# A decoder trunk with expert rows on TensorE: in the attention stages, the attention's matmuls are put ahead of the expert rows that are due

## What is computed

```python
h = rms(x) @ w_in                         # q, k, v, latents, convolution channels, gates
y_d = diff_attention(...)                 # 4 heads, two maps each: softmax(q0 k0) - lam * softmax(q1 k1), times v
y_m = mla(...)                            # 8 heads of 96, causal softmax, times v
y_c = short_conv(...)
x += (g0 * (y_d @ W_d) + g1 * (y_m @ W_m) + g2 * (y_c @ W_c)) @ w_out
# PEER: per token 8 heads x 16 experts, from 16384
act = gelu(sum(u_tab[expert] * hc))       # one dot per expert row
x += sum(gate * act * v_tab[expert])      # one weighted row per expert
x += sigmoid(rms(x) @ w_ple_gate) * (p @ w_ple_proj)
```

## Time and profile before

| | us |
|---|---|
| median of 3 runs | 3959.45 (3955.41 to 3967.53) |
| the profiled execution's own time | 3950.54 |
| its span in the trace | 3948.7 |
| TensorE, VectorE, ScalarE busy in it | 2984.8, 2583.0, 1447.1 |
| mean granted TensorE clock | 0.877 of full speed |

### The profile page before, as it was taken

How to read it: one execution, slowest core, us unless ns; L and a number is a source line. 1 busy time by engine, 2 the same in 40 slices (tenths; PEclk the granted TensorE clock), 3 DMA queues, 4 the chain that set the end, 5 groups by cost and what they waited for, 6 DMA issues and landing times.

```text
span 3948.7 us, 28848 instructions
## 1 busy us (share of the span) xinstructions
PE 2984.8 (76%) x8168; PEld 1518.6 (38%) x8168; DVE 2583.0 (65%) x5233; ACT 1447.1 (37%) x3974; POOL 1344.9 (34%) x1033
## 2 busy tenths in 40 slices
PE   8599669666898788766898789766898776655556
PEld 5254535333446335323445335333445432111112
DVE  1411677665567987675557987765566987777774
ACT  1320132556423333547323333546532343222222
POOL 0000044232333433433333444323332344555551
PEclk9789889888999899887999899888899988777778
DMA  4124289788898999988899999877899999999994
GB/s 167 56 85 155 96 354 412 259 332 295 328 390 351 366 369 413 372 332 310 341 393 354 374 375 415 349 297 295 308 393 352 366 386 408 421 422 422 422 422 197
DMA packets 182400, 1298.67 MB, mean 329 GB/s; under 512 B 20320, under 2 KB 21856, under 8 KB 26592
## 3 DMA queue, kind: packets, MB, share of 16 engines
q0 software_dynamic: 147456, 1073.81, 68.5%
q1 hardware_dynamic: 34784, 223.01, 14.3%
HBM read 1294.64 MB, written 2.10 MB: 328 GB/s over the span
## 4 chain that ended last, share of the span: by engine, by line
PE 25%; DMA 12%; DVE 10%; ACT 8%; issue 3%; POOL 1%; DVEq 0%; ACTq 0%; POOLq 0%
DMA ring<-in_uv,experts 12%; PE ps_sum L1273 9%; PE ps_act L1335 7%; DVE ring L1149 4%; PE ps_act L1379 3%; PE ps_dve L1514 2%; ACT L722 1%; PE ps_dve L1335 1%; DVE x L1158 1%; ACT diag L730 1%; ACT weight L724 1%; ACT area_e L518 1%; ACT L518 1%; ACT dots L722 1%; POOL ring L488 1%
## 5 line engine op out<-in xcount | busy, mean ns | idle before, releaser
L488 POOL DMA_INDIRECT ring<-in_uv,experts x1024 | 1342.4, 1311 | 2532.5 <-PE ps_sum L1273 989.7
L1273 PE MATMUL ps_sum<-ring,diag 128*128 128x512 f32 x2144 | 1295.8, 750 | 803.4 <-ACT diag L730 796.6
L1149 DVE SCALAR_TENSOR_TENSOR ring<-ring,h_ffn 128x1024 f32<-128x1024 f32 x1024 | 1230.7, 1218 | 189.8 <-DMA ring<-in_uv,experts 183.8
L1273 PEld LDWEIGHTS ps_sum<-ring,diag 128*128 128x128 f32 x2144 | 460.5, 230 | 1504.7 <-ACT diag L730 1074.8
L722 ACT ACTIVATE dots<-dots 128x1 f32<-128x1 f32 x1024 | 205.5, 201 | 1500.4 <-DVE ring L1149 1498.5
L1158 DVE SCALAR_TENSOR_TENSOR x<-ring,weight,x 128x1024 f32<-128x1024 f32 x488 | 625.1, 1281 | 192.5 <-ACT weight L724 192.4
L1335 PE MATMUL ps_act<-wt,area_h 128*128 128x512 f32 (+1 forms) x1536 | 662.5, 590 | 3.0 <-ACT area_h L504 2.5
L1335 PEld LDWEIGHTS ps_act<-wt,area_h 128*128 128x128 f32 x1536 | 293.9, 192 | 363.0 <-issue 357.8
L1379 PE MATMUL ps_act<-area_h,wt 128*128 128x256 f32 x1536 | 340.3, 381 | 5.1 <-ACT area_h L504 5.1
L724 ACT ACTIVATE weight<-dots,gate 128x1 f32<-128x1 f32 x1024 | 301.6, 295 | 33.3
L1379 PEld LDWEIGHTS ps_act<-area_h,wt 128*128 128x128 f32 x1536 | 292.1, 191 | 54.8 <-issue 9.1
(11 more groups left out here) (173 smaller groups left out, 2067.2 us busy)
## 6 DMA issues: line engine op xcount, KB each, us to landing
wt<-in_weights SPq DMA_DIRECT2D x192, 1024.0 KB, 8.5
ring<-in_uv,experts POOLq DMA_INDIRECT x1024, 10.8
wt<-in_weights SPq DMA_DIRECT2D x12, 512.0 KB, 8.9
wt<-in_weights SPq DMA_DIRECT2D x4, 768.0 KB, 8.6
x<-in_x SPq DMA_DIRECT2D x4, 512.0 KB, 5.0
area_y<-in_keys SPq DMA_DIRECT2D x4, 512.0 KB, 8.4
area_f<-in_keys SPq DMA_DIRECT2D x4, 512.0 KB, 9.6
area_f<-in_ffn_rows SPq DMA_DIRECT2D x4, 512.0 KB, 4.4
```

Of the source, the lines that this page charges most:

```text
L488: pool.indirect_dma_start(ring[:, row.slot, :], None, a[f"uv{row.step // 2}"][:, :], bass.IndirectOffsetOnAxis(ap=experts[:, row.step % 2, ...
L1149: dve.scalar_tensor_tensor(u, u, 1.0, h_ffn[:, row.tile, :], ALU.mult, ALU.mult, accum_out=dots[:, row.j:row.j + 1]).then_inc(dots_ready, 1)
L1273: ins = pe.matmul(ps_sum[:, b, :], diag[:, row.pe_before % DIAGS, :], ring[:, row.slot, D + b * 512:D + (b + 1) * 512], start=row.pe_first ...
```

## The change

A third list names the differential scores and products and all three MLA stages. For a stage in it, `serve` no longer adds `late` ahead of the stage; the main loop of TensorE adds it right behind the stage. The rule that a row which others can no longer wait for goes first (`needed`: 8 ring slots, 4 diagonals) stays. `diff_flip` stays in `ROWS_FIRST`. Only TensorE's order changes, and no instruction is added or removed on any engine.

```diff
+ROWS_LAST = ("diff_scores", "diff_pv", "mla_scores", "mla_flip", "mla_pv")
...
                 if name in ROWS_FIRST:
                     late.extend(fresh)
                     fresh.clear()
-                if name not in TICKS:
+                if name not in TICKS and name not in ROWS_LAST:
                     add_rows(late, len(late))
...
                     serve(name, units)
                     stage[name](at, d, *more)
+                    if name in ROWS_LAST:
+                        add_rows(late, len(late))
```

## The result

| | before | with the change |
|---|---|---|
| median, us | 3958.24 (3955.41 to 3967.53, 4 runs) | 3866.7 (3861.97 to 3872.23, 4 runs) |
| ratio, 95% interval | | 0.9765 (0.9744 to 0.9786) |
| profiled execution, us | 3950.54 | 3872.23 |

The change makes the kernel 2.35% faster, 93 us of 3958. The 93 us are the ratio's; the two medians lie 91.5 us apart. The forecast was 84 us less and 3875, with a range of 3838 to 3930.

The account below looks back on a forecast made before the run. In the MLA sweeps nothing is full, so a chain between engines sets the pace. Savings of 55 + 10 + 13 + 3 + 3 = 84 us from 3959.5 give 3875, range 3838 to 3930.

Parts of the forecast that it names:

- What bounds the kernel: MLA sweeps: no engine or DMA is full; a chain between engines sets the pace, 40.5% of step 1's being expert rows.
- Middle MLA heads: MLA heads 3 to 15: 7.1, 6.6 and 7.0 us a head against 8.9, 7.8 and 8.6, saving 55 us.
- MLA starts: Start of each MLA sweep: ScalarE's waits of 4.26, 1.76 and 4.53 us for the first maximum go, saving 10 us.
- Differential heads: Differential sweeps: 13 us saved in step 1, 3 at step 0's last scores, 3 at step 2's third scores.
- The remaining heads keep their order and their time: Other differential heads of steps 0 and 2: still wait for the flip behind rows, so no gain was counted.
- What moves back: Expert rows finish at most about 1.2 us later, returning ring slots and diagonals later; both covered, so no cost counted.
- 1 (transfers take over): Attention sweeps: the ring could run dry in bursts, leaving 50 us saved, time 3909; chance 0.15.
- 2 (ScalarE everywhere): MLA heads already at ScalarE's pace, only starts and differential heads gain: 29 us, time 3930; chance 0.04.
- 3 (given back): Mixing stage starts with an emptier ring and waits, 20 us a sweep, the whole gain: time 3955; chance 0.07.
- 4 (slower through the ring): Sweeps: late slot return makes dots wait for landings, costing 40 us at half of the rows, time 4000; chance 0.04.
- Two signs that missed: Step 1's MLA sweep: VectorE's waits for scores fall from 48.3 us to under 20; twelve middle heads take about 79.
- the case in which every such row runs at the lower clock: Middle MLA heads: every flip-stage row at half clock, 3.78 us, making the saving 34 us in place of 55.

Follow-up runs that it names:

- 9: The change with products put back behind their rows, so only scores and MLA flips pass: ratio 0.9826 to the kernel before.
- 3: The kernel before with only the differential and MLA scores passing their rows, flips and products staying behind theirs: ratio 0.9863, -54 us.
- 4: The kernel before with only MLA flips and both kinds of products passing their rows, scores staying behind theirs: ratio 0.9894, -42 us.
- 8: The change with the MLA flips put back behind their rows, scores and products passing: ratio 0.9761 to the kernel before.
- experiment 10: The change with no row made at the flip stage of either kind, those rows given to scores and products: ratio 0.955, median 3774.17 us.
- experiment 7: The change with seven ring slots in place of eight: ratio 0.9831 to the kernel before, 26 us more than the change.
- Experiment 1: The kernel before with only the three MLA stages putting rows last, differential stages as before: ratio 0.9802, -78 us.

## Why the prediction was right

**What bounds the kernel.** A chain between engines in the attention sweeps, nothing full: right. Only TensorE's order was changed, VectorE's and ScalarE's busy times stayed, and of the 78.4 us by which the profiled span is shorter 62.6 came out of TensorE's idle time.

**Middle MLA heads, 55 us.** Measured 51 in the traces: 22, 11 and 18 against 22, 14 and 19. The mechanism is right, but the sum was met partly by luck, since its two terms are both off, in opposite directions. The 18 heads whose scores stand behind a flip-stage row come 9.0 us after the head before, not 7.8. From the scores of the head before to that row it takes 6.3 us, not the 5.29 of the one turn that I read, and the row takes 2.9, not 2.6. The other 18 heads come after 5.0 us, not 6.0. That is less than ScalarE's busy time of 5.7 us a head, so their scores run ahead of ScalarE, and part of what they save is waited for at the next row. I had taken the two kinds of head as independent.

The wait that I had not read, ScalarE's for products, does close a loop: flip-stage row, product, its copy, exponential, diagonal, next row (timeline of 9). The prediction took the product out of the loop without a price. The expectation of 3 gave it one, 0.5 to 1 us of TensorE's time in 18 heads, and was too low with it: scores alone gain 54, not 65 to 75. Flips and products are worth the other 39, and 42 by themselves (4), so scores on one side and flips and products on the other add up, neither hiding the other. Flips and products do overlap: both taken back cost 39 (3), products alone 24 (9), MLA flips alone nothing (8). With 12 us of uncertainty on the 24, how much of it is ScalarE's loop and how much the product's own 9 to 18 us on TensorE is not shown.

**MLA starts, 10 us.** The waits went as forecast: from the last differential scores to the first of MLA the gain was 4.7, 1.9 and 4.3 us, 11 in all. Up to MLA head 3 it was 17, and the other 6 sit in step 1, where the first three heads gained 7.4 us on their way.

**Differential heads.** Step 1: 14 us against 13, and a pace of 6.3 to 8.0 us a head about the 7.7 forecast. Step 0's last head: 3 against 3. Step 2's third scores: nothing (+1.1) against 3. Up to the fourth scores 1.1 us were gained; the heads behind them, whose order is the same as before, took 2.2 us longer. "The remaining heads keep their order and their time": right, and experiment 10 shows that some 20 us in each of these two sweeps lay there.

**What moves back.** Rows returned their slots later and no dot waited in the sweeps: with seven slots the MLA sweeps still kept their length (7).

**The rivals.** 1 (transfers take over): not at this pace, though the DMA share of 0.91 to 0.96 was nearer than I had thought. In experiment 10 it is 1.00 in step 0, and even there no dot waited for a gather. 2 (ScalarE everywhere): refuted; heads went from 8.9 us to 7.1 and on to 5.8. 3 (given back): refuted by the table, -2 us behind the sweeps. 4 (slower through the ring): refuted by the result itself, and by experiment 7, where seven slots did not lengthen the MLA sweeps.

**Two signs that missed.** I said that VectorE's waits for scores in step 1 would fall under 20 us; they fell to 30.1, since scores are still behind the flip stage's row. And twelve heads there take 82 us, not 79. A third sign, expert rows under 30% of that sweep's chain, stays open, since no chain is shown there; in step 2 they fell from 31.9% to 22.3%. The other signs came: step 0's long heads stayed at 13 to 15 us, and step 3 kept its length.

**The clock and the table loads.** I counted nothing for the clock, and it gave a little. The granted clock of heads 3 to 15 went from 0.87, 0.79 and 0.85 to 0.88, 0.88 and 0.86. The mean record of a row matmul went from 750 to 739 ns over all 2144, 21.8 us of busy time in all, in these lines of the costliest groups, of before and of the change:

```profile
L1273 PE MATMUL ps_sum<-ring,diag 128*128 128x512 f32 x2144 | 1295.8, 750 | 803.4 <-ACT diag L730 796.6
```

```profile
L1274 PE MATMUL ps_sum<-ring,diag 128*128 128x512 f32 x2144 | 1274.0, 739 | 742.3 <-ACT diag L731 735.4
```

TensorE waited 61 us less for diagonals. The Trainium skill (TensorE: Matmul & The Clock Gate, "HAM oscillation — how this bites in real kernels") warns that waits between short groups of matmuls drop the clock each time, so that the group behind the wait starts at the lower level. The trace agrees in part: of the 18 rows that still stand alone ahead of middle heads' scores, mostly behind waits of 1.6 to 3.3 us, 13 took more than 1.98 us and one the full 3.78. Their mean of 2.9 us is far from 3.78, so the case in which every such row runs at the lower clock, with 34 us in place of 55, did not come.

Twelve heads of step 0 in experiment 10 hold 24 table loads in 69 us, with ScalarE busy 65.22 us, the loads of 1.28 us included and no drain among them. The 1.38 us of drain for each switch that the Trainium skill (ScalarE: Activation LUTs, "What ACT_TABLE_LOAD costs") gives would need 33 us, where 3.8 are left; the measurement decides, and here a switch costs its 1.28 us.

## What to carry to other kernels

Where two kinds of work share an in-order engine, look at what stands behind a wait in its queue rather than at how busy it is: put first what another engine needs and what is ready, and behind it what waits for a long chain. Then look for the piece whose input is made in the middle of the loop and let it be due elsewhere; the order and the due place are worth more together (178 us) than apart (93 and 51). Test the parts alone, and take them back one by one from the whole: scores against flips and products added up (54 and 42 against 93), while flips and products overlapped (nothing and 24 taken back singly, 39 together).

## What the runs showed that was not expected

**Identical sweeps differ by some 4 us, along with the granted clock.** Experiment 1 and the change have the same order on every engine in MLA. In step 2's heads 3 to 15 they took 81.4 and 85.3 us. The difference is that of the row matmuls' busy time, 40.4 and 44.5 us (first experiment 1, then the change):

```profile
L1274 PE MATMUL ps_sum<-ring,diag 128*128 128x512 f32 x73 | 40.4, 679 | 18.5 <-ACT diag L731 18.5
```

```profile
L1274 PE MATMUL ps_sum<-ring,diag 128*128 128x512 f32 x74 | 44.5, 731 | 17.0 <-ACT diag L731 17.0
```

at a granted clock of 0.92 and 0.86. In step 1 it was the other way, 85.4 us at 0.84 and 82.3 at 0.88. One sweep of one trace is therefore good to some 4 us at best, and it takes the medians over several runs to price a part at 10. The 99.9 us of scores alone in step 1, longer than before, came at a clock of 0.74; how much of it is the clock and how much the order was not settled.

**The start varies.** The stretch ahead of any attention beside rows varied by 12 us between executions (691 to 703), more than several of the effects measured here.
